# Key and value compression of the first mixer as one step on both column halves of the tensor engine, with a new order of steps

## The chip, the cores and the metric

The kernel runs on one core of one Trainium2 chip. The metric is the device time of one execution in microseconds, as the median of several runs; less is better.

## What is computed

The program takes 256 tokens of width 1024 through four transformer layers, each a mixer and a gated feed-forward network. The change touches the first mixer, which joins a retention with a sparse attention of eight heads. The sparse attention has three branches; one of them looks at compressed keys and values. Every compressed token covers 32 tokens and begins 16 after the one before it, so 256 tokens give 15 compressed ones for each of the two groups of heads:

```python
def nsa_compress(kv, pos_emb, w1, w2):
    B, G, S, d = kv.shape
    r = CMP_BLOCK // CMP_STRIDE
    parts = kv.reshape(B, G, S // CMP_STRIDE, CMP_STRIDE, d)
    n = S // CMP_STRIDE - r + 1
    blocks = jnp.concatenate([parts[:, :, j:j + n] for j in range(r)], axis=3)
    flat = (blocks + pos_emb.astype(jnp.float32)).reshape(B, G, n, CMP_BLOCK * d)
    return jax.nn.gelu(flat @ w1.astype(jnp.float32)) @ w2.astype(jnp.float32)
...
    k_cmp = nsa_compress(kvh(kc), pos_k, w1_k, w2_k)
    v_cmp = nsa_compress(kvh(vc), pos_v, w1_v, w2_v)
```

With a head width of 64, `flat` has 2048 columns, `w1` is 2048x64 and `w2` is 64x64. Keys and values have weights of their own.

## The kernel before

**The stream of products.** The program is eight stages: mixers are the even ones, feed-forward networks the odd ones. All large weights pass as one stream of chunks of 128x1024 floats or less. SP loads a chunk into one of four `raw` buffers; ACT copies it to `whi`, rounded (`split`, L2047); POOL subtracts to get the rest, `wlo` (`lo`, L2347), in pieces of 256 columns here; and PE multiplies the activations with both (`product`, L1063, L1064 and L1070). The split of a chunk waits for the end of the sixth chunk before it, and the load of a chunk for the low part of the fourth before it. A block of output columns is four chunks here (three in the third block, which is 280 wide). Its units are sorted by the half of the tokens, so four successive units use four chunks, and the next four use them again.

**The order of the rest.** All other work is cut into steps, called by two letters: `TT` turns keys, `TC` copies them, `CA` is the product with `w1`, `CB`, `CE` and `CD` are the gelu (DVE, ACT, DVE), `CF` is the product with `w2`, `CG` its copy, `SC` are scores, `MK` their maxima, `EX` exponentials, `NW` normed weights, `TR` their turn, `AV` the product with the values, `EV` the eviction of a block, `GD` and `GE` the gates. A table of numbers, `PLAN`, says after which unit of the stage each step stands; each engine walks through the table and issues the steps that are its own, in that order. `@0`, `@1`, `@2` behind a step names its lane of PSUM: A[0], A[1] or G[1]. So the table fixes what each engine has in front of what, and a step whose input isn't there stops all that stands behind it on its engine.

**The compression before.** `keys_copy` (L2173, L2174) writes the turned keys and values into `Z`, 128 partitions with six groups of 256 columns, three each for keys and values (the third holds the position terms). `compress_in` is issued twice, for keys (`kind` 0) in G[1] and for values in A[0], each as 16 matmuls of the 64 columns of `w1c` with 45 columns of `Z` that lie 16 floats apart:

```python
z = Z[:, 3 * kind:3 * kind + 3, 2 * m:2 * m + 225:16]
wt = w1c[:, kind, 64 * m:64 * m + 64]
o = e.matmul(tile[0:64, 0:45].rearrange("p (g i) -> p g i", g=3), wt, z, start=m == 0, stop=m == 15)
```

Both results stand in partitions 0 to 63, and each has its own gelu there. A matmul in float32 shows as two records in the trace.

Of the kernel before, what the change touches and what calls it, by code (L numbers as in the profile page):

```python
# [286 lines left out]
40: MK 0 1 0; NA 2 0 0; EX 0 1 0; EX 1 1 1
41: WH 2 0 0; NW 0 1 0; NW 1 1 1
43: WL 2 0 0; TR 0 1 0; CPA 0 1 0; TR 1 1 1; SC 0 1 1 @2; MK 0 1 1; AV 0 1 0
44: CPA 1 1 1; NO 0 1 0; EX 0 1 1; CPV 1 1 1; SC 2 1 0 @0; AV 1 1 1  # L290
45: EV 5 0; MK 2 1 0; NO 1 1 1; EX 2 1 0
46: NW 2 1 0; SC 2 1 1 @1; EV 5 1; TR 2 1 0; NW 0 1 1
47: MK 2 1 1; CPA 2 1 0; EX 2 1 1
48: NA 2 1 0; AV 2 1 0; WH 2 1 0; TR 0 1 1
49: NW 2 1 1; WL 2 1 0
50: EV 6 0; GS 0; CPA 0 1 1; TR 2 1 1; CPV 2 1 1; R2A 0; R2V 0; CPA 2 1 1
51: R1 0 @0
53: R3 0; AV 0 1 1; AV 2 1 1; R4 0; NO 0 1 1; NA 2 1 1; WH 2 1 1; WL 2 1 1; R5 0; EV 6 1; R1 1 @1; GS 1
54: R2A 1; GT 0; R2V 1; GT 1; R6 0; R3 1; R7 0
55: R4 1; R8 0  # L300
57: R5 1; R6 1; MT 2 @0
58: MH 2; R7 1; ML 2
59: R8 1
61: MT 3 @1
62: MH 3
# [6 lines left out]
0: -RES 1 1; -RES 0 1  # L312
1: -SQ 0 1; -SQ 1 1; -XT 0 1; -XH 0 1
# [5 lines left out]
11: -RS 0; DR 0; SI 0 0; DR 1  # L319
13: RV; RM  # L320
14: HM 0 0; HM 0 1
15: HH 0 0
16: HT 0 1; HL 0 0; GX 1; GA 1
17: HT 0 0; SG 1; HL 0 1; HH 0 1; UX 1; HU 1
# [287 lines left out]
24: EV 2 1
25: EX 0 1; TR 0 0
26: KT 1 @0; NW 0 1; KA 1; CPA 0 0
27: KV 1; TR 0 1; EV 3 0; CPV 0 1; SC 1 0 @0; CPA 0 1; AV 0 0; WH 0 0; TBM 2; WH 0 1; WL 0 0; MK 1 0; WL 0 1
28: SC 1 1 @1; AV 0 1; MK 1 1
30: LB 3; EX 1 1; EX 1 0
# [8 lines left out]
42: EX 2 1; TR 2 0; CPA 2 0; NW 2 1; MK 3 0
44: TR 2 1; SC 3 0 @1; EV 5 0; EX 3 0; AV 2 0
45: CPV 2 1; NW 3 0
46: WH 2 0; CPA 3 0; CPA 2 1; WL 2 0; EV 5 1
47: TR 3 0  # L630
48: SC 3 1 @0; AV 3 0; WH 2 1; AV 2 1; WH 3 0
# [55 lines left out]
70: RES 0 0; BN 0 0  # L687
74: RES 0 1; BN 0 1
92: RES 1 0; BN 1 0; AG 0
93: RS 0  # L690
94: AP 0 0
95: AP 1 0; RES 1 1; BN 1 1; AG 1; RS 1; AP 0 1; AP 1 1
# [41 lines left out]
def program(nc, a, out):  # L734
    ctx = ExitStack()
    with ctx:
# [40 lines left out]
        w2c = sb("w2c", [64, 256], F, e0)  # L777
# [1636 lines left out]
```

## Time and profile before

| | |
|---|---|
| runs | 1279.97, 1278.13 and 1278.50 us; median 1278.5 us |
| the profiled execution | 1279.67 us, of which 1277.9 us is the span from the first to the last instruction |
| PE busy | 1263.6 us (99%), weight loads 1059.1 us (83%) |
| POOL, ACT, DVE busy | 1030.2, 768.9 and 494.0 us |
| mean granted TensorE clock | 0.997 |

A profile has a page of sums, a chain of waits (who released whom, followed back from the last instruction), a list of waits by engine, a timeline of each engine, and a table of stretches with busy times and granted clock. PE is the tensor engine's matmul side and PEld its weight loads, DVE the vector engine, ACT the scalar engine, POOL the GpSimd engine, SP the engine that issues the loads. The end of a matmul is modelled: a row's time reaches over the start of the next, so the pace of a row of many records is its time less that of one record, divided by their number less one.

### The profile page before, as it was taken

To read this page: it belongs to the slowest core of one execution; us is meant where nothing else is said; L and a number is where in the kernel's file an instruction comes from. 1 tells how busy PE (TensorE), PEld (TensorE's weight loads), DVE (VectorE), ACT (ScalarE), POOL (GpSimd) and SP (SyncE) were. 2 spreads that over 40 slices of the span, in tenths; PEclk is the share of its full clock that TensorE was granted. 3 is DMA by queue.
4 is the path that set the end of the run, shared out by engine and by line. 5 is a ranking of instruction groups with operands and counts; after the bars stand their busy time and mean duration, and the time that the engine had idled before them with its cause. 6 is when DMAs were issued, how large, how long until landed. Compare 5 with 4: busy or idle time off the path is not lost.

```text
span 1277.9 us, 20392 instructions
## 1 busy us (share of the span) xinstructions
PE 1263.6 (99%) x7594; PEld 1059.1 (83%) x7594; DVE 494.0 (39%) x1096; ACT 768.9 (60%) x1481; POOL 1030.2 (81%) x874
## 2 busy tenths in 40 slices
PE   8999999999999999999999999999999999999997
PEld 7877888888887887888888888888888888888886
DVE  3465424331168862433104565133203345233302
ACT  7656676654688877666445675466534565556631
POOL 6666789878977668988889787798889878799874
PEclk9999999999999999999999999999999999999999
DMA  8443466556544336656556444576565644476652
GB/s 287 155 132 108 140 222 215 191 170 185 183 162 133 121 110 201 197 187 192 177 188 200 151 146 151 184 223 218 182 196 171 227 149 132 153 247 210 191 173 82
DMA packets 63122, 224.97 MB, mean 176 GB/s; under 512 B 7344, under 2 KB 7984, under 8 KB 63024
## 3 DMA queue, kind: packets, MB, share of 16 engines
q1 hardware_dynamic: 62736, 223.57, 54.3%
q8 instruction: 61, 1.00, 0.3%
q14 instruction: 37, 0.30, 0.1%
q10 hardware_dynamic: 288, 0.10, 0.0%
HBM read 222.59 MB, written 1.05 MB: 175 GB/s over the span
## 4 chain that ended last, share of the span: by engine, by line
PE 95%; DVE 2%; ACT 2%; issue 1%; DMA 0%; SPq 0%; DVEq 0%; ACTq 0%
PE G L1063 18%; PE G L1064 17%; PE G L1070 17%; PE G L1089 10%; PE A L1089 10%; PE A L1092 5%; PE G L1092 5%; PE A L1201 1%; PE A L1118 1%; PE A L1237 1%; DVE MX L1942 1%; PE A L1261 1%; DMA X<-in_x 0%; PE G L1201 0%; PE A L1361 0%
## 5 line engine op out<-in xcount | busy, mean ns | idle before, releaser
L2347 POOL TENSOR_TENSOR wlo<-raw,whi 128x256 fp32r<-128x256 f32 (+2 forms) x866 | 1020.6, 1215 | 230.1 <-ACT whi L2047 229.2
L2047 ACT ACTIVATE whi<-raw 128x1024 fp32r<-128x1024 f32 x403 | 422.0, 1057 | 194.7 <-PE G L1070 152.5
L1063 PE MATMUL G<-whi,xx 128*128 128x512 f32 (+1 forms) x560 | 225.9, 404 | 0.3
L1064 PE MATMUL G<-whi,xx 128*128 128x512 f32 (+1 forms) x560 | 217.3, 389 | 0.0
L1070 PE MATMUL G<-wlo,xx 128*128 128x512 f32 (+1 forms) x560 | 171.7, 388 | 0.0
L1089 PE MATMUL G<-xx,whi 128*128 128x512 f32 x576 | 144.6, 393 | 0.0
L1089 PE MATMUL A<-xx,whi 128*128 128x512 f32 x576 | 144.5, 393 | 0.0
L1063 PE MATMUL G<-whi,hh 128*128 128x512 f32 x352 | 137.5, 391 | 0.0
L1064 PE MATMUL G<-whi,hl 128*128 128x512 f32 x352 | 137.1, 389 | 0.0
L1063 PEld LDWEIGHTS G<-whi,xx 128*128 128x128 f32 x560 | 105.4, 188 | 24.5 <-issue 4.9
L1070 PEld LDWEIGHTS G<-wlo,xx 128*128 128x128 f32 x560 | 104.8, 188 | 22.5
L1064 PEld LDWEIGHTS G<-whi,xx 128*128 128x128 f32 x560 | 105.6, 188 | 18.3
L1089 PEld LDWEIGHTS A<-xx,whi 128*128 128x128 f32 x576 | 103.8, 189 | 18.8
L1089 PEld LDWEIGHTS G<-xx,whi 128*128 128x128 f32 x576 | 103.6, 189 | 18.5
L1070 PE MATMUL G<-wlo,hh 128*128 128x512 f32 x352 | 108.4, 389 | 0.0
L1092 PEld LDWEIGHTS G<-xx,wlo 128*128 128x128 f32 x576 | 78.6, 190 | 5.6
L1092 PEld LDWEIGHTS A<-xx,wlo 128*128 128x128 f32 x576 | 78.6, 190 | 5.6
L1092 PE MATMUL A<-xx,wlo 128*128 128x256 f32 x576 | 80.3, 282 | 0.0
L1092 PE MATMUL G<-xx,wlo 128*128 128x256 f32 x576 | 80.3, 282 | 0.0
L1070 PEld LDWEIGHTS G<-wlo,hh 128*128 128x128 f32 x352 | 66.1, 188 | 13.9
L1063 PEld LDWEIGHTS G<-whi,hh 128*128 128x128 f32 x352 | 66.1, 188 | 13.4
L1064 PEld LDWEIGHTS G<-whi,hl 128*128 128x128 f32 x352 | 66.1, 188 | 13.4
(394 smaller groups left out, 1502.2 us busy)
## 6 DMA issues: line engine op xcount, KB each, us to landing
raw<-in_g SPq DMA_DIRECT2D x88, 512.0 KB, 3.7
raw<-in_u SPq DMA_DIRECT2D x88, 512.0 KB, 3.7
raw<-in_d SPq DMA_DIRECT2D x88, 512.0 KB, 4.0
raw<-in_w_h SPq DMA_DIRECT2D x32, 512.0 KB, 3.6
raw<-in_w_e SPq DMA_DIRECT2D x24, 512.0 KB, 3.7
raw<-in_w_a SPq DMA_DIRECT2D x24, 512.0 KB, 3.7
raw<-in_w_b SPq DMA_DIRECT2D x24, 512.0 KB, 3.5
raw<-in_w_eo SPq DMA_DIRECT2D x8, 512.0 KB, 3.5
```

The lines of the kernel that those rows point to most:

```text
L1063: e.matmul(o, sh[:, kt, xs], whi[h][:, ws], start=u.first and j == 0, stop=False)
L1064: e.matmul(o, sl[:, kt, xs], whi[h][:, ws], start=False, stop=False)
L1070: m = e.matmul(o, sh[:, kt, xs], wlo[h][:, ws], start=False, stop=u.stop and final)
L1089: e.matmul(o[:, :], whi[h][:, 128 * kt:128 * kt + 128], xx[:, kt, :], start=kt == 0, stop=False)
L1092: m = e.matmul(o[:, 0:256], wlo[h][:, 128 * kt:128 * kt + 128], xx[:, kt, 0:256], start=False, stop=kt == u.kts[-1])
L1118: m = e.transpose(A[t][:, 512 * b + 128 * i:512 * b + 128 * i + 128], X[:, t, 512 * b + 128 * i:512 * b + 128 * i + 128], ident)
L1201: m = e.matmul(tile[:, at:at + nk], qs[i], ks[i], start=not mask, stop=True, skip_group_check=True)
L1237: m = e.transpose(tile[0:kp, (i * nb + b) * 128:(i * nb + b) * 128 + 128], s[:, 2 * i if key[0] == 4 else i, 128 * b:128 * b + kp], ident)
L1261: m = e.matmul(heads4(tile[64 * g:64 * g + 64, 0:256], 2), v, wt[:, g:4:2, b, :], start=b == 0, stop=b == nb - 1, skip_group_check=True)
L1942: m = e.tensor_copy(mixed[rows, :, :, rows], blocks[rows])
L2047: e.activation(whi[c % NH][:, 0:n], raw[c % NR][:, 0:n], ACT.Copy).then_inc(s_hi, 1)
L2347: m = e.tensor_tensor(wlo[c % NH][:, i:j], raw[c % NR][:, i:j], whi[c % NH][:, i:j].bitcast(F), ALU.subtract)
```

## The change

The compression is one step with one key. Its 32 matmuls alternate between keys, which write partitions 0 to 63, and values, which write 64 to 127 of the same PSUM tile. The gelu runs once on 128 partitions. The second weights of the values lie in partitions 64 to 127, and their result goes to the second bank of G[1]. Then the table is new for stages 0, 1, 6 and 7 (in stages 1 and 7 a few steps move by one unit, in stage 6 some steps of the attention). Stages 2 to 5 are the same.

```diff
-18: TT 2 @1; CA 0 @2; CB 0; CA 1 @0; TC 2; EV 2 0; CE 0; CD 0; CB 1; MK 1 0 0
-19: CD 1; CG 0; SC 1 0 0 @1
-20: CE 1
-21: CG 1; GD; MK 0 0 1; EV 2 1; GE; EX 1 0 0; TC 3; EX 0 0 1; CF 1; CF 0
-23: TT 3 @0; SC 0 0 1 @2
+18: TT 2 @1; CB 0; TC 2; EV 2 0; CD 0; CE 0; MK 1 0 0
+19: CA 0 @2; CG 0; EV 2 1
+21: MK 0 0 1; EX 1 0 0; GD; GE; SC 1 0 0 @1; TC 3; CF 0; EX 0 0 1; TT 3 @0
+22: SC 0 0 1 @2
...
-                    e.dma_start(w2c[:, 0:64], a["cw2k"]).then_inc(d_cw, 16)
-                    e.dma_start(w2c[:, 64:128], a["cw2k"]).then_inc(d_cw, 16)
-                    e.dma_start(w2c[:, 128:192], a["cw2v"]).then_inc(d_cw, 16)
+                    e.dma_start(w2c[0:64, 0:64], a["cw2k"]).then_inc(d_cw, 16)
+                    e.dma_start(w2c[0:64, 64:128], a["cw2k"]).then_inc(d_cw, 16)
+                    e.dma_start(w2c[64:128, 0:64], a["cw2v"]).then_inc(d_cw, 16)
...
             def compress_in(key):
-                _, kind = key
                 tile, _ = lane_of("CA", key)
                 lane_free("CA", key)
                 e.wait_ge(d_cw, 16 * CW_LOADS)
-                e.wait_ge(S["TC"], nth("TC", 0, kind))
+                for kind in range(2):
+                    e.wait_ge(S["TC"], nth("TC", 0, kind))
                 e.wait_ge(S["MB"], nth("MB", 0))
                 for m in range(16):
-                    z = Z[:, 3 * kind:3 * kind + 3, 2 * m:2 * m + 225:16]
-                    wt = w1c[:, kind, 64 * m:64 * m + 64]
-                    o = e.matmul(tile[0:64, 0:45].rearrange("p (g i) -> p g i", g=3), wt, z, start=m == 0, stop=m == 15)
+                    for kind in range(2):
+                        z = Z[:, 3 * kind:3 * kind + 3, 2 * m:2 * m + 225:16]
+                        o = e.matmul(tile[64 * kind:64 * kind + 64, 0:45].rearrange("p (g i) -> p g i", g=3),
+                                     w1c[:, kind, 64 * m:64 * m + 64], z, start=m == 0, stop=m == 15)
                 o.then_inc(S["CA"], 1)
 
             def compress_out(key):
-                _, kind = key
                 tile, w = lane_of("CA", key)
-                x = w[0][0:64, 0:30]
+                x = w[0][:, 0:30]
                 e.wait_ge(S["CD"], nth("CD", *key))
-                if kind == 0:
-                    m = e.matmul(tile[:, 0:30], w2c[:, 0:128], x, start=True, stop=True)
-                else:
-                    for g in range(2):
-                        m = e.matmul(tile[0:15, 64 * g:64 * g + 64], x[:, 15 * g:15 * g + 15], w2c[:, 128:192],
-                                     start=True, stop=True)
+                e.matmul(tile[:, 0:30], w2c[0:64, 0:128], x[0:64], start=True, stop=True)
+                for g in range(2):
+                    m = e.matmul(tile[0:15, 512 + 64 * g:576 + 64 * g], x[64:128, 15 * g:15 * g + 15], w2c[64:128, 0:64],
+                                 start=True, stop=True)
                 m.then_inc(S["CF"], 1)
...
-                x, u, bias = w[0][0:64, 0:30], tile[0:64, 64:94], w[0][0:64, 96:97]
+                x, u, bias = w[0][:, 0:30], tile[:, 64:94], w[0][:, 96:97]
...
-                x, u, v = w[0][0:64, 0:30], tile[0:64, 64:94], tile[0:64, 96:126]
+                x, u, v = w[0][:, 0:30], tile[:, 64:94], tile[:, 96:126]
...
-                if kind == 0:
-                    e.tensor_copy(CK[:, 0:30], tile[:, 0:30]).then_inc(S["CG"], 1)
-                else:
-                    e.tensor_copy(CK[0:15, 64:192], tile[0:15, 0:128]).then_inc(S["CG"], 1)
+                e.tensor_copy(CK[:, 0:30], tile[:, 0:30])
+                e.tensor_copy(CK[0:15, 64:192], tile[0:15, 512:640]).then_inc(S["CG"], 1)
```

The table moves instructions at three places that matter here. The first is PE between the third unit of the third block and the fourth (units 18 and 19 of the stage). `Z,w1c` is the product with `w1`; `whi,xx` and `wlo,xx` are units. Before:

```order
L1159 MATMUL A<-CN,PJ 128x128 x2
L1172 MATMUL G<-Z,w1c 64x45 x16
L1172 MATMUL A<-Z,w1c 64x45 x16
L1063 MATMUL G<-whi,xx 128x280
L1064 MATMUL G<-whi,xx 128x280
```

And now:

```order
L1152 MATMUL A<-CN,PJ 128x128 x2
L1056 MATMUL G<-whi,xx 128x280
L1057 MATMUL G<-whi,xx 128x280
...
L1063 MATMUL G<-wlo,xx 128x280 x3
L1165 MATMUL G<-Z,w1c 64x45 x32
```

The product with `w1` moved back by one unit, and its two rows became one.

The second place is PE at the end of the third block, with the product with `w2` (`W,w2c` and `w2c,W`) and the scores of a later branch (`MB,IB` and `KT,QT`). Before:

```order
L1196 MATMUL A<-MB,IB 128x2x128 x2
L1201 MATMUL A<-KT,QT 128x128 x4
...
L1070 MATMUL G<-wlo,xx 128x280 x2
L1184 MATMUL A<-w2c,W 15x64 x2
L1181 MATMUL G<-W,w2c 128x30
L1063 MATMUL G<-whi,xx 128x512
```

And now:

```order
L1063 MATMUL G<-wlo,xx 128x280 x2
L1187 MATMUL A<-MB,IB 128x2x128 x2
L1192 MATMUL A<-KT,QT 128x128 x4
L1173 MATMUL G<-W,w2c 128x30
L1175 MATMUL G<-w2c,W 15x64 x2
L1152 MATMUL A<-CN,PJ 128x128 x2
L1056 MATMUL G<-whi,xx 128x512
```

The scores came later by two units, to stand directly ahead of the product with `w2`, and the turn of the last keys came earlier, directly behind it.

The third place is ACT around the copies into `Z`, where `whi<-raw` is the split of a chunk. Before:

```order
L2060 ACTIVATE PJ<-G,SM 128x512
L2047 ACTIVATE whi<-raw 128x1024
L2173 ACTIVATE Z<-G 64x256
...
L2174 ACTIVATE Z<-A 64x255
L2047 ACTIVATE whi<-raw 128x1024 x2
L2176 ACTIVATE KT<-A 128x256
L2060 ACTIVATE PJ<-G,SM 128x280
L2183 ACTIVATE G<-G 64x30
L2047 ACTIVATE whi<-raw 128x1024
L2183 ACTIVATE A<-A 64x30
```

And now:

```order
L2048 ACTIVATE PJ<-G,SM 128x512
L2161 ACTIVATE Z<-A 64x256
...
L2162 ACTIVATE Z<-A 64x255
L2035 ACTIVATE whi<-raw 128x1024 x3
L2164 ACTIVATE KT<-A 128x256
L2048 ACTIVATE PJ<-G,SM 128x280
L2171 ACTIVATE G<-G 128x30
L2048 ACTIVATE PJ<-G,SM 128x280
```

The split of the first chunk of the fourth block moved from ahead of the eight copies to behind them; the exponential of the gelu is one. On POOL and SP no row moves.

## Rows read from the trace of the kernel before

**Rows 1.** The page: span, shares of the chain that ended last.
```profile
span 1277.9 us, 20392 instructions
...
PE 95%; DVE 2%; ACT 2%; issue 1%; DMA 0%; SPq 0%; DVEq 0%; ACTq 0%
```

**Rows 2.** The two longest waits of PE (us in total, times, longest).
```profile
PE A L1118 <- DMA X<-in_x: 2.2, 2, 1.1
PE A L1337 <- ACT QK L2272: 1.8, 1, 1.8
```

**Rows 3.** Timeline of PE, 36 to 49 us: start us, us, line, out<-in, shape, count.
```profile
36.49 2.73 PE L1172 MATMUL G<-Z,w1c 128*64 128x45 f32 x32
39.04 2.71 PE L1172 MATMUL A<-Z,w1c 128*64 128x45 f32 x32
41.68 0.40 PE L1063 MATMUL G<-whi,xx 128*128 128x280 f32 x1
...
42.95 0.39 PE L1196 MATMUL A<-MB,IB 128*128 128x256 bf16 x2
43.27 0.71 PE L1201 MATMUL A<-KT,QT 64*128 64x128 f32 x8
43.92 0.40 PE L1063 MATMUL G<-whi,xx 128*128 128x280 f32 x1
...
45.18 0.30 PE L1063 MATMUL G<-whi,xx 128*128 128x280 f32 x1
...
46.05 0.39 PE L1184 MATMUL A<-w2c,W 64*15 64x64 f32 x4
...
46.71 0.50 PE L1063 MATMUL G<-whi,xx 128*128 128x512 f32 x1
...
48.22 0.39 PE L1063 MATMUL G<-whi,xx 128*128 128x512 f32 x1
```

**Rows 4.** Timeline of PE, three later stretches: halves, then strips of the array.
```profile
382.26 0.51 PE L1361 MATMUL G<-W 128*32 128x32 f32 x35
...
1021.93 1.09 PE L1266 MATMUL G<-W,PJ 128*64 128x128 f32 x16
1022.95 0.50 PE L1063 MATMUL G<-whi,xx 128*128 128x512 f32 x1
```

**Rows 5.** Timeline of DVE, 39 to 49 us: the gelu of the keys, the gates.
```profile
39.25 0.15 DVE L1554 COPY W<-G 64x1 f32<-64x1 f32 x1 [12.49 <-PE G L1172]
...
41.69 0.18 DVE L1575 TENSOR_TENSOR W<-G,W 64x30 f32<-64x30 f32 x1
...
47.12 1.39 DVE L1589 TENSOR_SCALAR SM<-PJ 128x24 f32<-128x24 f32 x2
```

**Rows 6.** Timeline of ACT, 33 to 42 us: splits and copies into Z.
```profile
33.49 1.05 ACT L2047 ACTIVATE whi<-raw 128x1024 fp32r<-128x1024 f32 x1
34.44 0.36 ACT L2173 ACTIVATE Z<-G 64x256 f32<-64x256 f32 x1
...
37.17 0.38 ACT L2174 ACTIVATE Z<-A 64x255 f32<-64x255 f32 x1
37.57 2.00 ACT L2047 ACTIVATE whi<-raw 128x1024 fp32r<-128x1024 f32 x2
...
40.88 0.17 ACT L2183 ACTIVATE G<-G 64x30 f32<-64x30 f32 x1 [0.51 <-DVE G L1565]
```

**Rows 7.** Timeline of POOL, 34 to 50 us: the low parts of the weights.
```profile
34.62 2.81 POOL L2347 TENSOR_TENSOR wlo<-raw,whi 128x256 fp32r<-128x256 f32 x4 [1.54 <-ACT whi L2047]
38.71 11.17 POOL L2347 TENSOR_TENSOR wlo<-raw,whi 128x256 fp32r<-128x256 f32 x16 [1.28 <-ACT whi L2047]
```

**Rows 8.** Stretches of 2 us: busy PE, PEld, DVE, ACT, POOL, then PEclk.
```profile
406.00:408.00 2.00, 1.83 (x9) 1.66 (x10) 1.97 (x5) 1.97 (x4) 0.88 (x2) 0.79 0.00 0
408.00:410.00 2.00, 2.00 (x31) 1.18 (x33) 1.09 (x4) 1.06 (x3) 1.93 (x3) 0.50 0.02 4
410.00:412.00 2.00, 2.00 (x52) 1.72 (x44) 1.23 (x4) 2.00 (x4) 0.00 (x0) 0.85 0.48 133
```

More of the change, by code:

```diff
@@ L287 @@
[L287 to L305, printed above, removed]
+37: NW 2 0 0; CPA 1 1 0; AV 2 0 1; RO 1 1; NO 1 1 0; AV 1 1 0; TR 2 0 0
+39: WH 2 0 1; NA 2 0 1; WL 2 0 1; CPA 2 0 0; SC 1 1 1 @1; SC 0 1 0 @0; MK 1 1 1; AV 2 0 0
+40: EX 0 1 0; NA 2 0 0; MK 0 1 0; EX 1 1 1
+41: NW 0 1 0; NW 1 1 1; WH 2 0 0
@@ new lines @@
+42: TR 0 1 0; CPA 0 1 0
+43: WL 2 0 0; AV 0 1 0; TR 1 1 1
+44: SC 2 1 0 @0; SC 0 1 1 @2; CPA 1 1 1; NO 0 1 0; AV 1 1 1; CPV 1 1 1
+45: EV 5 0; EX 2 1 0; MK 2 1 0; MK 0 1 1; EX 0 1 1; NO 1 1 1; SC 2 1 1 @1; TR 2 1 0
+46: NW 2 1 0; NW 0 1 1; EV 5 1; MK 2 1 1; CPA 2 1 0; AV 2 1 0
+48: EX 2 1 1; NA 2 1 0; TR 0 1 1
+49: WL 2 1 0; NW 2 1 1; WH 2 1 0
+50: EV 6 0; GS 0; TR 2 1 1; CPA 0 1 1; CPV 2 1 1; R2A 0; R2V 0; CPA 2 1 1
+51: R4 0; R1 0 @0
+53: NO 0 1 1; R3 0; AV 0 1 1; AV 2 1 1; NA 2 1 1; WH 2 1 1; WL 2 1 1; R5 0; EV 6 1; R1 1 @1; GS 1
@@ L306 @@
+54: R2A 1; R2V 1; GT 0; R7 0; R3 1; R6 0; GT 1; R4 1
+55: R8 0
+56: R5 1; R6 1; MT 2 @0
+57: MH 2
+58: ML 2
+59: R8 1; R7 1
+61: MH 3; MT 3 @1
 63: ML 3
-65: RES 0 0; SQ 0 0; XT 0 0; RES 1 0
-66: XH 0 0; XT 1 0; XL 0 0; XH 1 0
+65: RES 0 0; XT 0 0; RES 1 0; SQ 0 0
+66: XH 0 0; XL 0 0; XT 1 0
+67: XH 1 0
 68: XL 1 0
@@ L318 @@
 10: -SQ 1 0
[L319 to L324, printed above, removed]
+11: DR 0; -RS 0; SI 0 0; DR 1
+13: RV; HM 0 0; RM
+15: HM 0 1; HH 0 0
+16: GX 1; HL 0 0; GA 1; HT 0 0
+17: SG 1; UX 1; HL 0 1; HT 0 1; HH 0 1; HU 1
 18: HB 1; HW 1; GX 2; GA 2
@@ L606 @@
 13: EV 1 0
-15: EV 1 1; SC 0 1 @2; SC 0 0 @1
-16: MK 0 0
-17: MK 0 1; EX 0 0
+15: EV 1 1; SC 0 1 @2; SC 0 0 @1; MK 0 0; EX 0 0
+17: MK 0 1
 19: NW 0 0; LB 2
 20: EV 2 0
[L612 to L617, printed above, removed]
+21: EX 0 1
+24: EV 2 1; TR 0 1
+25: TR 0 0
+26: KT 1 @0; NW 0 1; CPA 0 0; KA 1
+27: KV 1; CPA 0 1; EV 3 0; CPV 0 1; AV 0 0; AV 0 1; SC 1 0 @0; WH 0 0; WH 0 1; TBM 2; WL 0 0; MK 1 0; WL 0 1; SC 1 1 @1; MK 1 1
+30: EX 1 1; LB 3; EX 1 0
 33: EV 3 1; NW 1 1
@@ L622 @@
 37: KV 2; WL 1 1
-39: SC 2 1 @2; SC 2 0 @0; EV 4 1; MK 2 0; KT 3 @1
+39: SC 2 0 @0; SC 2 1 @2; EV 4 1; MK 2 0; KT 3 @1
 40: EX 2 0
 41: KA 3; MK 2 1; NW 2 0; KV 3
[L626 to L631, printed above, removed]
+42: EX 2 1; TR 2 0; CPA 2 0; NW 2 1
+43: MK 3 0; EV 5 0
+45: CPV 2 1
+46: SC 3 0 @1; EX 3 0; AV 2 0; TR 2 1; WH 2 0; CPA 2 1; CPA 3 0; NW 3 0; WL 2 0; EV 5 1
+48: TR 3 0; SC 3 1 @0; AV 3 0; WH 2 1; AV 2 1; WH 3 0
 49: MK 3 1
 50: WL 2 1
-51: EX 3 1; WL 3 0; NW 3 1
+51: WL 3 0; EX 3 1; NW 3 1
 58: TR 3 1; RES 0 0
@@ L686 @@
 52: HB 18; HW 18; TBL
[L687 to L690, printed above, removed]
+74: RES 0 0; RES 0 1; BN 0 1
+75: BN 0 0
+91: RES 1 0
+92: BN 1 0; AG 0; RS 0; AP 1 0
 94: AP 0 0
-95: AP 1 0; RES 1 1; BN 1 1; AG 1; RS 1; AP 0 1; AP 1 1
+95: RES 1 1; BN 1 1; RS 1; AG 1; AP 0 1; AP 1 1
 """,
@@ L776, in program @@
         w1c = sb("w1c", [128, 2, 16 * 64], F, e0)
-        w2c = sb("w2c", [64, 256], F, e0)
+        w2c = sb("w2c", [128, 128], F, e0)
         CK = sb("CK", [128, 512], F, e0)
@@ L1550, in gelu_argument @@
                 tile, w = lane_of("CA", key)
-                x, u, bias = w[0][0:64, 0:30], tile[0:64, 64:94], w[0][0:64, 96:97]
+                x, u, bias = w[0][:, 0:30], tile[:, 64:94], w[0][:, 96:97]
                 k = -2.0 * (2.0 / np.pi) ** 0.5
                 e.wait_ge(S["CA"], nth("CA", *key))
-                e.tensor_copy(bias, tile[0:64, 30:31]).then_inc(s_dve, dv.up())
+                e.tensor_copy(bias, tile[:, 30:31]).then_inc(s_dve, dv.up())
                 own()
-                e.tensor_scalar(x, tile[0:64, 0:30], bias, None, ALU.add).then_inc(s_dve, dv.up())
+                e.tensor_scalar(x, tile[:, 0:30], bias, None, ALU.add).then_inc(s_dve, dv.up())
                 own()
```

59 lines of the change are left out of this document (26 added, 33 removed).

## The prediction

> **What bounds the kernel now.** I read the page first: the span is 1277.9 us, and the chain that ended last runs through PE for 95% of it [rows 1]. PE is busy for 1263.6 us of the span. The list of PE's waits is short: the first loads, 2.2 us in all, and one wait for copies by ACT in the third stage, 1.8 us [rows 2]. None lies in the first mixer once it runs. So a microsecond that PE does not have to issue is a microsecond of time, work that goes from DVE or ACT is worth nothing by itself, and a new wait of PE costs its full length. That is why the timeline of PE comes next [rows 3], and then, for every step that PE will wait on, the timelines of DVE, ACT and POOL [rows 5, 6, 7].
>
> **The product with the first weights, before.** It holds PE from 36.49 to 41.68 us, 5.19 us for 64 records [rows 3]. The pace of a record is (2.73 - 0.26) / 31 = 0.080 us, where 0.26 is about one record's own time. So 63 paces are 5.0 us, and leaving for the next unit the rest.
>
> **The same, on two halves.** A record on the left half and one on the right may run side by side. The trace has this form: 16 records of 128 columns on alternating halves take 1.09 us, so their pace is (1.09 - 0.27) / 15 = 0.055 us, or 0.109 for a pair [rows 4]. Four strips of 32 columns show it more strongly: 35 records in 0.51 us are a pace of (0.51 - 0.20) / 34 = 0.009 us [rows 4], or 0.28 ns a column, less than the 0.42 ns of one clock at 2.4 GHz, so streams must run side by side there. In our case each half still has to take its own 32 records, and the only pace seen for such a record is 0.080. A pair then costs 0.080, and 32 pairs 2.55 us. Ends: the 16 records of the halves keep PE from 1021.93 to 1022.95, 1.02 us, against 16 x 0.055 = 0.87, so 0.15 us [rows 4]. Together 2.70 us, and **the saving is 5.19 - 2.70 = 2.5 us**. Bounds: without any overlap 64 x 0.080 + 0.15 = 5.3 us, no saving at all; if a half were as quick per column as the pairs of 128, 0.109 x 45/128 = 0.038 for a pair, 1.2 + 0.15 us, a saving of 3.8. I take 2.5, since the single stream is the nearest row and it has the same stride and the same weights.
>
> There is a rule that speaks against this part. The Trainium skill, page "TensorEngine Tiling (Array Packing)", section "Performance Considerations", says that every matmul carries some 60 cycles of overhead, that few columns are no quicker than 60, and that one should not take the factor from a dimension that is already small. Our 45 columns are such a dimension. If that overhead were paid one record after the other, the product would stay at 5.3 us and the time at 1278.6 us. By that rule, the trace does not agree for the strips, which stream 32 columns at 0.009 us a record [rows 4].
>
> **Joined and parted steps.** A run of row or column halves costs PE its ends: eight records of the scores at a pace of (0.71 - 0.27) / 7 = 0.063 are 0.50 us, but they hold it from 43.27 to 43.92, 0.65 us [rows 3]. So 0.15 us a run. The product with the second weights stood alone from 46.05 to 46.71 [rows 3] and now follows the scores directly: one run fewer. One product with the values stands alone now (one more), and in stage 6 two runs of halves became one (one fewer). Net -0.15 us, with bounds of -0.4 and +0.2.
>
> **Off the path.** DVE drops 9 small operations and ACT one exponential; PE never waited for them, so 0. The loads of w2c are the same three; SP and POOL keep their order: 0. Stages 1 and 7 move steps by a unit with no wait of PE near: 0.
>
> **What PE may now wait for.** Four places.
> - The product with w1 needs all eight copies into Z. They took from 34.44 to 37.55 us behind a split that began at 33.49 [rows 6]; without that split ahead they begin some 0.2 us sooner and end at 37.3. PE comes there one unit later than before, at 36.49 + 1.27 = 37.7 (a unit of nine records holds 41.68 to 42.95) [rows 3]. Slack 0.3 us.
> - The gelu took DVE and ACT from 39.25 to 41.87 = 2.62 us [rows 5]. PE has ahead of the second product: a unit of nine (1.27), a unit of six (46.05 - 45.18 = 0.87) and scores (43.92 - 42.95 = 0.97), 3.1 us, less the tail of the last matmul, 0.26 [rows 3]. Slack 0.2 us. ACT must be free when the exponential comes: its three splits after 37.3 end at 40.3, and a copy and an eviction at 41.1; the exponential comes at about 42.2. Free.
> - The split of the first chunk of the fourth block ends at 38.3 us, behind the copies, and not at 34.5. POOL stood idle for it before; now its four chunks of four pieces, at 11.17 / 16 = 0.70 us a piece [rows 7], are done at 38.3 + 11.2 = 49.5. PE begins that block at 46.71 - 2.4 = 44.3, needs up to 1.51 us a unit [rows 3], and comes to the low part of the fourth chunk at about 44.3 + 4.2 + 0.5 (scores) + 0.9 = 49.9. Slack 0.4 us, where it was over 5.
> - The clamp of the gates, 1.39 us [rows 5], comes behind the maxima of the second scores on DVE. Between 0 and 1.39 us of it may show; I expect nearer 0, as the first turn of weights stands three units later.
>
> Three slacks of 0.2 to 0.4 us and one unknown: I add 0.2 us, bounds 0 and 1.4.
>
> **Sum.** -2.5 - 0.15 + 0.2 = -2.4 us. Against the profiled execution (1279.67 us; 1.8 of it lies outside the span) that is 1277.3. The median of the runs shown is 1278.5, 1.2 lower. What differs is likely the clock: after PE's wait of 1.8 us the granted clock fell, 0.79, 0.50 and 0.85 of 2.4 GHz in three stretches of 2 us [rows 8], a loss of 0.4 + 1.0 + 0.3 = 1.7 us, and the two lower runs are 1.2 and 1.5 us under the profiled one. The Trainium skill, page "TensorE: Matmul & The Clock Gate", Part 1, has two such levels, half and full rate; the trace agrees with its 0.50 in one stretch. So I take the median as the base: **1276.1 us**, 0.19% less. A difference under 0.2%, 2.6 us, can't be told from none, and the forecast lies just inside.
>
> **Rivals.**
> - *The halves do not overlap for this operand.* Z is read 16 floats apart, and 0.080 us for 45 columns is slow beside 0.109 for a pair of 128. If the stride sets the pace and both halves share the reading, a pair costs 0.16 and nothing is gained: 1276.1 + 2.5 = 1278.6 us. For it: no strided stream runs in halves in this trace. Against it: the strips read four streams at once [rows 4]. The Trainium skill, page "SBUF — State Buffer", section "Door 1", says that elements in a new 16-byte line each pay a penalty; that explains 0.080, and does not say whether two streams pay it twice. Chance 0.14; with the fixed overhead above, 0.03 more.
> - *The clock is at half speed in the median run.* The wait of 1.8 us stays [rows 2], and a fall after it costs 1.7 us: 1277.8 us. It may have been in one run of three before. Chance 0.18.
> - *Slower: the weights come late.* The mechanism is POOL's debt. It starts 3.7 us later into four chunks that it works at 2.8 us each, while PE uses them at 1.4 us each [rows 3, 7]. If a split waits for ACT by more than the slack of 0.4 us, PE waits for the low part in the fourth unit, the next loads (each bound to an old low part) come late too, and each of the four blocks behind pays: 4 x 1 us, and with a fall of the clock 1.7: 1276.1 + 5.7 = 1281.8. It decides from 5.0 us of waits on, since 2.4 are saved. Against it: POOL is idle later in every block, when chunks wait for PE. Chance 0.07.
>
> **How the numbers follow.** The forecast has 0.58, the rivals 0.17, 0.18 and 0.07. The forecast's own cases reach from 1275.9 without any wait to 1276.6; its centre is 0.16 us from the bound of 0.2%, so I give 0.38 of its 0.58 to faster and 0.20 to the same, for the base may be a little high or low. The first rival is no change (0.17), the second too (0.15 of 0.18, 0.03 faster). So faster 0.41, same 0.52, slower 0.07. The range reaches down to 1274.8 (the saving of 3.8 us on the product instead of 2.5) and up to 1279.3 (the first rival with half of the bound of the waits, 0.7); outside lie the slower rival and parts of the others, under 0.2.
>
> **What would show it.** Right: one row of 64 records on halves in G, about 2.7 us long, with pairs of starts; no wait of PE for Z, for the gelu or for a low part between 36 and 60 us; the fourth block beginning at 44.3. Wrong: a row of about 5 us (first rival), a wait of PE for DVE at the product with w2, or a granted clock under 1.00 elsewhere. If POOL's debt counts, PE's waits name POOL's line near 50 us.

## The result and the profile after

The changed kernel takes **1281.39 us** in the median of 16 executions (1280.44 to 1287.19) where the kernel before takes 1279.15 (16 executions, 1278.13 to 1281.61). The ratio is 1.0023, with a 95% interval of 1.0016 to 1.0030: slower by 0.2%, where 1276.1 us was forecast. Two of the sixteen lie at 1286.3 and 1287.2, and one at 1283.8; the highest of the kernel before is 1281.61. The profiled execution took 1281.39 us, and its span is 1279.6 us, 1.7 more than before [rows 1].

Below, line numbers are those of the changed kernel: 7 to 9 less than before in PE's part, 9 to 12 less in those of DVE, ACT and POOL.

The edit itself did what it was meant to. PE's timeline of the changed kernel, the same stretch as [rows 3]:

```profile
37.59 2.83 PE L1165 MATMUL G<-Z,w1c 128*64 128x45 f32 x64
40.34 0.40 PE L1056 MATMUL G<-whi,xx 128*128 128x280 f32 x1
...
43.27 0.30 PE L1173 MATMUL G<-W,w2c 64*128 64x30 f32 x2
43.50 0.39 PE L1175 MATMUL G<-w2c,W 64*15 64x64 f32 x4
...
44.02 0.48 PE L1056 MATMUL G<-whi,xx 128*128 128x512 f32 x1
```

The product with w1 holds PE from 37.59 to 40.34, 2.75 us and not 5.19, and the next block begins at 44.02 where it was to begin at 44.3. Compared product by product, PE is 2.9 us ahead of the kernel before at 52 us and still at 404 us, in the middle of stage 2; under 0.1 us of that stood already ahead of the product with w1. Then it loses it all. PE's longest waits in the changed kernel, which answer to [rows 2]:

```profile
PE A L1328 <- ACT QK L2260: 5.9, 1, 5.9
PE G L1097 <- DVE PJ L1414: 1.0, 1, 1.0
PE A L1111 <- DMA X<-in_x: 1.0, 1, 1.0
```

The wait for the copies QK was 1.8 us and is 5.9. The stretches of 6 us around it in the changed kernel (busy PE, PEld, DVE, ACT, POOL, then PEclk), where [rows 8] showed 0.79, 0.50 and 0.85 in stretches of 2 us:

```profile
400.00:406.00 6.00, 1.52 (x7) 0.94 (x5) 5.90 (x18) 3.48 (x10) 0.00 (x0) 1.00 0.22 82
406.00:412.00 6.00, 4.55 (x31) 3.51 (x35) 4.32 (x10) 4.21 (x14) 2.79 (x4) 0.53 0.00 1
412.00:418.00 6.00, 6.00 (x139) 5.16 (x131) 3.81 (x10) 5.23 (x7) 3.40 (x5) 0.90 0.26 90
418.00:424.00 6.00, 6.00 (x158) 5.17 (x146) 4.05 (x11) 4.77 (x18) 6.00 (x10) 1.00 0.63 182
```

The two stretches behind the wait miss 6 x (0.47 + 0.10) = 3.4 us of full clock, twice the 1.7 us of [rows 8]. Of the 1.7 us more, 1.1 show in the shift of the products behind it. So the account is -2.9 (stage 0), +4.1 (the wait), +1.1 (the clock) and -0.6 (stage 6, where the new order has fewer ends of runs; which edit there gives it was not tried apart) = +1.7 us, the difference of the spans.

Whose work is late? The chain of waits of the changed kernel, from 390 us to PE's restart (start, us, what), names it:

```profile
389.84 0.32 DVE G L1835
390.15 0.29 issue
390.45 8.47 DVE MX L1930
398.94 0.22 DVE MX L1930
...
402.48 0.10 ACT lf L2245
...
405.40 2.00 ACT QK L2260 x11
407.41 0.04 issue
407.45 0.58 PE A L1328
```

L1930 (1942 before) is `diagonal_blocks`, called DB here: VectorE copies four blocks of 32 partitions x 128 elements from one SBUF tile (DG) to another (MX). One of them takes 8.47 us. The line by itself, before and then changed (ns min/median/max, first and last start):

```profile
L1942 DVE COPY MX<-DG x16: 202/683/2929, 393.3 to 465.9; 32x128 f32<-32x128 f32 x16
```

```profile
L1930 DVE COPY MX<-DG x16: 202/223/8475, 390.4 to 468.2; 32x128 f32<-32x128 f32 x16
```

It was in the trace of before, unread: sixteen equal copies whose shortest takes 202 ns and whose longest 2929. Beside them GpSimd makes low parts of weights in one unbroken run. Its timeline, before and changed:

```profile
382.16 19.57 POOL L2347 TENSOR_TENSOR wlo<-raw,whi 128x256 fp32r<-128x256 f32 x28 [3.52 <-ACT whi L2047]
```

```profile
379.30 19.55 POOL L2335 TENSOR_TENSOR wlo<-raw,whi 128x256 fp32r<-128x256 f32 x28 [3.53 <-ACT whi L2035]
```

A piece takes 19.55 / 28 = 0.70 us, four make a slice. In the changed kernel the copy comes at 390.45, where the 17th piece begins (379.30 + 16 x 0.698 = 390.47), is held for twelve pieces, and ends at 398.92, just behind the run (398.85). Before, it came at the same piece (393.30, against 382.16 + 16 x 0.699 = 393.34) and was held for four only, to 396.23. Everything before that point has moved by the same 2.85 us, and yet the one copy is held for three times as long. That is what the experiments are about.

### The profile page after: what moved, and what is told of

Read it like the earlier page. It is cut to its first block, busy times and chain, and to the rows that moved or that the text cites. A ratio compares the mean times of both kernels' runs of the same rounds, so it can differ in the third digit from the quotient of the medians.

```text
span 1279.6 us, 20380 instructions
## 1 busy us (share of the span) xinstructions
PE 1262.3 (99%) x7594; PEld 1058.7 (83%) x7594; DVE 497.1 (39%) x1087; ACT 769.7 (60%) x1480; POOL 1029.9 (80%) x874
## 4 chain that ended last, share of the span: by engine, by line
PE 92%; ACT 2%; DVE 2%; POOL 2%; DMA 1%; issue 1%; SPq 0%; DVEq 0%; ACTq 0%
PE G L1056 17%; PE G L1057 17%; PE G L1063 17%; PE G L1082 10%; PE A L1082 10%; PE A L1085 5%; PE G L1085 5%; POOL wlo L2335 1%; PE A L1192 1%; PE A L1111 1%; PE A L1228 1%; DVE MX L1930 1%; ACT whi L2035 1%; PE A L1252 1%; DMA X<-in_x 0%
```

## The experiments

Each time is the median of a kernel's executions, taken on the same chip as a series of the kernel before. Theory A: the copy can't run beside GpSimd's subtractions, and its length is PE's wait. Rivals: the copy only reports a delay that ScalarE or a DMA makes; the length of the hold is a matter of the phase of arrival.

### Another form of the copy: e1 to e4

```
-  m = e.tensor_copy(mixed[rows, :, :, rows], blocks[rows])
+  m = e.tensor_tensor(mixed[rows, :, :, rows], blocks[rows], blocks[rows], ALU.max)
```

In e1 and e2 for all four blocks, in e3 and e4 for the first block only.

> The changed kernel, with the four copies of the step DB on VectorE (the diagonal blocks, 32 partitions x 128 elements, from SBUF to SBUF) written as the maximum of the block and itself: same values, same place in the order. In the changed kernel's profile these four take 9.17 us in stage 2 (one of them 8475 ns), and it ends when GpSimd's unbroken run of 28 subtractions ends; TENSOR_TENSOR steps of the same stretch run beside GpSimd at their usual length. Theory A (a plain copy inside SBUF cannot run beside a GpSimd instruction, and this copy holds up PE): the four take about 1 us, TensorE's wait of 5.9 us for QK in stage 2 is under 0.5 us, its clock doesn't fall at 417 us, and the time is 1281.4 - 5.9 - 3.4 = 1272.1 (1271.5 to 1274). Theory B (the wait comes from the late slice of weights or from ScalarE's evictions, and the copy only reports it): the wait stays between 4 and 6 us and the time between 1280.5 and 1282. Theory C (the four are slow in any form, since GpSimd takes the reads): four instructions of some 0.7 us each and more, time 1276 to 1281.

> The kernel before with the same edit of DB. There the four took 5.03 us, PE waited 1.8 us, and the clock was at half for 3.4 us. Theory A: the wait of 1.8 us and the clock's fall both go: 1279.15 - 1.8 - 1.7 = 1275.6 (1275.2 to 1277.5). Against the changed kernel with this edit it then is 2.5 to 2.9 us slower, since the saving of the change (2.85 us in the shift of every product of stages 0 and 1) is no longer given back. Theory B: 1278.5 to 1280, and the changed kernel with the edit stays slower than this one. Theory C: 1277 to 1279.

> The changed kernel with only the first of DB's four blocks as a maximum, the other three still as copies. The first copy then comes some 0.2 us later, in the middle of a GpSimd subtraction and not 8 ns ahead of one. Theory A with chance (a copy gets in only when it happens to be first at the end of a GpSimd instruction): the time held up changes by whole subtractions of 0.70 us; it may be anything from 0.7 to 8.5 us, and the time lies between 1274 and 1282, and the three copies' excess and PE's wait go together one for one. Theory D (the copy always waits till GpSimd's run of 28 ends, whatever its arrival): the first copy again ends at the run's end, about 398.9 us, and the time is 1281 to 1282.

> The kernel before with only the first of DB's four blocks as a maximum. There the first copy waited for four subtractions (2.93 us) and each later one for one (0.69 us). Theory A with chance: a different number of whole subtractions; 0.2 us of arrival can change the time by several us in either direction (1275.5 to 1283). Theory D: the three copies end with GpSimd's run, at about 401.7 us, PE's wait grows by about 4 us and the time is 1283 to 1285. A smooth dependence (the copy costs what it did less one of four): 1278.3 to 1279.

Measured: e1 1287.22 us (1282.22 to 1288.56), e2 1280.11, e3 1287.15, e4 1278.54, beside 1279.65 before. All expectations of theory A for e1 and e2 were missed. In e3 the hold ends with GpSimd's run, as theory D said, but the time is 5 us over its 1282; in e4 it does not, and the time is that of the smooth dependence. The line in e1's profile says why theory A was missed:

```profile
L1930 DVE TENSOR_TENSOR MX<-DG x16: 261/288/8549, 396.8 to 474.2; 32x128 f32<-32x128 f32 x16
```

A maximum of two operands in SBUF is held exactly as the copy is. The twelve and the four come again with their kernels: e1 and e3 (changed) have 8549 ns, e2 and e4 (before) 3006 and 2994. So this change of the operation does not end the hold. The phase was not varied by it: in all four the first instruction comes within 0.03 us of the start of the 17th piece, as in the two kernels without the edit. What settles the phase is e11 and e14, further down.

e1 and e3 are also 6 us longer than the changed kernel, through something earlier. PE's second wait in e1, and what DVE and POOL do ahead of it:

```profile
PE A L1228 <- DVE W L1678: 4.0, 1, 4.0
```

```profile
47.42 5.59 DVE L1577 TENSOR_SCALAR SM<-PJ 128x24 f32<-128x24 f32 x2
```

```profile
39.00 13.89 POOL L2335 TENSOR_TENSOR wlo<-raw,whi 128x256 fp32r<-128x256 f32 x20 [4.30 <-ACT whi L2035]
```

That is the clamp of the gates, a tensor_scalar inside SBUF that took 1.39 us in [rows 5]. In e1 its first instruction is held for 5507 ns, till GpSimd's run of twenty pieces in stage 0 ends (39.00 + 13.89 = 52.89 us), and the weights of the local attention wait behind it. PE waits 4.0 us, and behind that the granted clock is 0.50 from 56 to 58 us and 0.67 from 58 to 60, a loss of 1.7: together the 6 us. It would explain the few executions of the changed kernel that lie some 5 us higher (none of them has a profile); e13 and e15 put that to the test. DB comes 340 us behind the clamp, so the edit of e1 and e3 cannot be what holds it; what makes five of six executions of e1, and all five of e3, have the long hold was not found.

### A form with one input: e5 and e6

```
-  m = e.tensor_copy(mixed[rows, :, :, rows], blocks[rows])
+  m = e.tensor_reduce(mixed[rows, :, :, rows], blocks[rows].unsqueeze(4), X_AX, ALU.add)
```

> The changed kernel with DB's four copies written as a reduction over an axis of length 1 (one SBUF input, same values). The maximum form of the first call was held up just like the copy (8549 ns), while the TENSOR_REDUCE of the blocks that runs in the same stretch, from SBUF to SBUF beside GpSimd's subtractions, takes 520 ns and is never longer. Theory A, made narrower (a plain copy or tensor_scalar inside SBUF and any VectorE instruction with two SBUF inputs is held while GpSimd runs; one with a single input outside these is not): the four take about 1 us together, PE's wait for QK in stage 2 is under 0.5 us in place of 5.9, its clock doesn't fall behind it, and a run in which the clamp of the gates (a tensor_scalar inside SBUF, 47 us) is not held long comes to 1281.4 - 5.9 - 3.4 = 1272.1 (1271.5 to 1274.5); a run in which it is held for 5.5 us, as in e1, is 4 to 5 us longer. Theory E (it is ScalarE's or the DMA's timing that makes PE wait, and any form of DB shows it): the wait stays over 4 us and the time at 1281.

> The kernel before with the same reduction for DB. Theory A: PE's wait of 1.8 us for QK goes and so does the half clock behind it: 1279.15 - 1.8 - 1.7 = 1275.6 (1275 to 1277). The changed kernel with this edit is then 2.5 to 3.5 us faster than this one, which is what the change saves by itself. Theory E: 1278.5 to 1280.

Measured: e5 **1272.96 us** (ratio to before 0.9957, 0.9942 to 0.9972), e6 1276.26 us (0.9978, 0.9968 to 0.9987). The line in e5:

```profile
L1930 DVE TENSOR_REDUCE MX<-DG x16: 261/276/284, 396.7 to 464.9; 32x128 f32<-32x128 f32 x16
```

Sixteen instructions between 261 and 284 ns, beside the same run of GpSimd. PE's wait for QK is gone from both lists, and the granted clock is 1.00 from 406 to 424 us in both. In the kernel before that is worth 2.9 us in the medians (2.3 against the 1278.58 taken beside e6) and 3.6 in PE's products (a shift of +0.3 us ahead of it and -3.3 behind): 3.1 right behind the wait, for its 1.8 and most of the 1.7 of clock, and 0.5 more by 500 us. In the changed kernel it is worth 1281.39 - 1272.96 = 8.4 us. The profiled execution of e5 is the one of its seven that took 1278.94 us: in it the clamp is held for 5492 ns, PE waits 4.0 us behind that, and the clock falls behind the wait as in e1, which is the 6 us over the others. Theory A holds in its narrower form, and the rival that blames ScalarE or a DMA falls: neither was touched.

The Trainium skill, page "SBUF — State Buffer", section "Who interferes with whom", has this rule: VectorE and GpSimd share one pair of SBUF ports, which one instruction locks as a whole; a copy or tensor_scalar in a two-port mode wants it, so does a VectorE instruction with two SBUF inputs while GpSimd reads, and a tensor_reduce never does. The runs agree in all four forms: copy 8475 ns, tensor_scalar 5507, maximum 8549, reduction at most 284. How many of GpSimd's instructions the waiting side has to let pass, the rule does not say.

### Four pieces or twelve: e7, e8, e11, e14

Before the change, ScalarE's high part of the sixth slice of that run was ready at 395.98 us (it began at 394.93, below) and GpSimd took it up at 396.10. Changed, it was ready at 392.85, and GpSimd took it up at 393.25, 0.4 us later. The difference is a hole of 0.29 us ahead of ScalarE's activation L2244, which the kernel before has and the changed one has not. ScalarE's timeline, before and changed:

```profile
393.76 0.60 ACT L2244 ACTIVATE W<-G 128x512 f32<-128x512 f32 x1 [0.29 <-issue]
394.39 0.60 ACT L2246 ACTIVATE G<-W 128x512 f32<-128x512 f32 x1
394.93 2.13 ACT L2047 ACTIVATE whi<-raw 128x1024 fp32r<-128x1024 f32 x2
```

```profile
391.80 1.05 ACT L2035 ACTIVATE whi<-raw 128x1024 fp32r<-128x1024 f32 x1
393.15 1.06 ACT L2035 ACTIVATE whi<-raw 128x1024 fp32r<-128x1024 f32 x1 [0.29 <-PE G L1063]
```

The expectation of e11 takes the 0.29 us in the changed kernel for the same hole at a later place. The rows name another cause: before, nothing that the profile shows ends it ("issue"); changed, the split of the seventh slice waits for the end of a unit on PE. In all traces of the changed kernel and its variants the activation that answers to L2244 starts 12 to 16 ns behind the one ahead of it, and in all of the kernel before 289 or 290 ns.

Theory G: a held instruction gets in only where GpSimd itself must stop, if only for an instant; here that is the boundary between two slices, if the next high part is just ready. e7 and e8 make GpSimd stop at every slice, e11 makes the high part late by more work on ScalarE, e14 stops GpSimd at this one boundary (slice 123).

e7 and e8, and e14 with the condition `if c == 123` ahead of the new wait:

```
 e.wait_ge(s_hi, c + 1)
+e.wait_ge(s_lo, c)
```

e11:

```
+for i in range(0, 896 if c == 123 else 0, 128):
+    e.activation(whi[c % NH][:, i:i + 128], raw[c % NR][:, i:i + 128], ACT.Copy)
+i = 896 if c == 123 else 0
-e.activation(whi[c % NH][:, 0:n], raw[c % NR][:, 0:n], ACT.Copy).then_inc(s_hi, 1)
+e.activation(whi[c % NH][:, i:n], raw[c % NR][:, i:n], ACT.Copy).then_inc(s_hi, 1)
```

> The changed kernel, DB as it was; GpSimd waits before each slice's subtractions until its own subtractions of the slice before are done, so that its run has a gap every four pieces (2.8 us). In the traces so far VectorE's held copy got in only where a slice's high part was ready 0.12 us before GpSimd needed it (before) and not where it was ready 0.4 us ahead (changed). If GpSimd's unbroken issue is what keeps the copy out: no held instruction is longer than 3.0 us; DB takes at most 5 us as before, the clamp of the gates at most 3; time 1274 to 1278. If the number of subtractions that it waits for has another cause: one of 8.5 us again, and 1281 to 1282.5.

> The kernel before with the same wait of GpSimd for its own last slice. The copy there was already let in after one slice (2.93 us), so by the theory nothing changes but the gaps of some 0.05 to 0.1 us per slice on GpSimd: 1278 to 1280. Where GpSimd's throughput were the bound of a stage it would be slower: over 1281.

> The changed kernel, DB and clamp as they were, with more work on ScalarE: the high part of one slice (the one whose split began at 391.80 us and ended at 392.85, 0.4 us before GpSimd began its low part at 393.25) is made in eight pieces, so that it ends 0.3 to 0.6 us later. Theory G (the held copy gets in only where GpSimd must itself wait, or nearly, for a slice's high part; in the kernel before that part was ready 0.12 us ahead because of a hole of 0.29 us in ScalarE's issue, which in the changed kernel lies one instruction later): the first copy of DB is held for four subtractions (2.8 to 3.0 us) and not for twelve (8.5), DB takes 5 us, PE's wait falls from 5.9 to 1.8 us, its half clock from 6.8 to 3.4 us, and the kernel with more work is 4 to 6 us faster: 1275.5 to 1277.5. Rival (the number of subtractions depends on something else, such as the phase of the arrival): 8.5 us again and 1281 to 1282.

> The changed kernel with one wait more and nothing else: before the slice whose subtractions begin at 393.25 us in stage 2 GpSimd waits for its own subtractions of the slice before. Theory G (unbroken issue over that boundary keeps the copy out): the first copy of DB is held for four subtractions, 2.8 to 3.0 us, in place of twelve; PE's wait falls from 5.9 us to 0.8 to 1.8; the lower level of the times is 1274 to 1276.5, that is 5 to 7 us under the changed kernel, for a wait that costs GpSimd under 0.2 us. Rival: the copy is held for twelve again and the time stays at 1281 to 1282.

Measured: e7 1276.83 us, e8 1280.31; e11 1274.30, with seven executions at 1273.8 to 1274.3 and five at 1279.65 to 1279.9; e14 three at 1274.4 to 1275.0 and nine at 1280.4 to 1281.8. The step DB in VectorE's timelines of e11 and e14, which took 9.17 us in the changed kernel:

```profile
390.70 4.07 DVE L1930 COPY MX<-DG 32x128 f32<-32x128 f32 x4
```

```profile
390.60 4.50 DVE L1930 COPY MX<-DG 32x128 f32<-32x128 f32 x4
```

GpSimd's run in the same two:

```profile
379.56 13.98 POOL L2338 TENSOR_TENSOR wlo<-raw,whi 128x256 fp32r<-128x256 f32 x20 [3.51 <-ACT whi L2038]
393.88 5.66 POOL L2338 TENSOR_TENSOR wlo<-raw,whi 128x256 fp32r<-128x256 f32 x8 [0.34 <-ACT whi L2038]
```

```profile
379.41 19.79 POOL L2337 TENSOR_TENSOR wlo<-raw,whi 128x256 fp32r<-128x256 f32 x28 [3.51 <-ACT whi L2035]
```

The first copy is held for 2922 and 2887 ns, four pieces, as theory G said. And it comes at the same phase as ever, by the 17th piece: 390.70 us against 379.56 + 16 x 0.699 = 390.74 in e11, 390.60 against 379.41 + 16 x 0.698 = 390.58 in e14. With the phase kept and the hold gone from twelve pieces to four, the phase falls as the reason. In e11 more work on ScalarE makes the kernel 7.1 us faster at its lower level (1281.39 against 1274.3); in e14 one wait of GpSimd, which lengthens its run of 28 pieces by 0.24 us (19.79 for 19.55), takes PE's wait down to 1.3 us, and the lower level is 6.4 to 7 us under the changed kernel. The expected 5 to 7 us of e14 were right. The 4 to 6 of e11 were exceeded: PE's wait is 0.8 us and not 1.8, since two of the three later copies take 0.22 us and not 0.69, and the clock does not fall behind it. The median of e14 is still 1280.81 us, no better than the kernel before, for nine of its twelve executions are at the upper level. e7 shows that waits at every slice end both holds (the longest DB copy 731 ns, the clamp 0.49 us in all) but cost some 4 us elsewhere (e7 against e5 3.9, e8 against e6 4.1): in e7 PE waits 0.9 us for a low part at 28 us and loses 2 us more for VectorE at 500 and 975 us. e8 is 0.3 us over the 1280 that were expected at most.

So a stop of GpSimd ends the hold: that is shown. That the 0.12 us against the 0.4 make the difference between the two kernels has no test but e11, where the high part was so late that GpSimd stood still for 0.34 us; before, no stop shows in its row. What makes the hole of 0.29 us ahead of L2244 was not tried.

### The clamp: e9, e10, e13, e15

e9 and e10 have DB as in e5, and the clamp with its output given as 3 x 8 columns.

```
-  e.tensor_scalar(gates[:, 24 * t:24 * t + 24], ...
+  e.tensor_scalar(gates[:, 24 * t:24 * t + 24].rearrange("p (a b) -> p a b", a=3), ...
```

> The changed kernel with DB as a reduction (as in e5) and with the clamp of the gates given its output as 3 x 8 columns and its input as 24: the same values in the same place, in a form of the operands that two ports could not halve. In e5 one of seven runs was at 1278.9 and had the clamp held for 5.5 us; the other six were at 1272.7 to 1273.0. Theory A (both are one mechanism): both clamps take 0.15 to 0.25 us each, PE's wait of 4.0 us for the local attention's weights is never seen, and every run lies between 1272.3 and 1273.5, 6 us under the changed kernel with 8 us off the upper end of its scatter. Rival F (the clamp is held in this form too, so its being held is not a matter of the second port): it shows 0.65 us and more, and some runs at 1278 to 1279 again.

> The kernel before with the same two edits. The clamp was held for 0.69 and 0.78 us there, never for longer in the profiles so far, and PE waited for nothing behind it: 1276.3 as e6 (1275.8 to 1276.6). The pair with e9 gives the change alone, without the held instructions: 3.3 us (2.9 to 3.6), of which 2.85 us in stage 0 and the rest in stage 6.

Measured: e9 1273.29 us with one of nine executions at 1280.0, e10 1276.25. The clamp in e9 still has 648 and 783 ns: rival F was right that this form is held too. Three columns of eight lie side by side, so they may have become one of 24 again on the way to the chip; that is open. As a pair, e10 and e9 give the change alone: 1276.25 - 1273.29 = **3.0 us** in the medians, and 3.35 us in the last products of the two traces, of which 2.75 come from stage 0 and 0.6 from stage 6.

e13 has DB as in e5 and lets GpSimd stop at the pieces beside the clamp; e15 has VectorE as it was and only pauses of GpSimd, those of e13 and that of e14 (123 is added to the first list).

```
+  if c in (14, 15, 16):
+      e.wait_ge(s_lo, c)
   for i, j in zip(cuts, cuts[1:]):
       m = e.tensor_tensor(wlo...)
+      if c in (14, 15) and j < n:
+          m.then_inc(s_pl, 1)
+          e.wait_ge(s_pl, 3 * (c - 14) + j // 256)
```

> The changed kernel with DB as a reduction, and with GpSimd waiting for its own last piece before each of the next ones in the three slices of stage 0 beside which the clamp of the gates comes (from 46.7 to 53 us), and nowhere else. Theory A: the clamp is held for at most one piece (0.9 us for each of its two instructions), PE never waits for the local attention's weights, no execution lies at the upper level of 1278 to 1280 and all lie within 1272.5 to 1273.8. If the upper level has another cause, one execution in four to nine is again 6 us longer.

> The changed kernel with VectorE's work untouched and pauses of GpSimd alone: the one of e14 in stage 2, and those of e13 beside the clamp of the gates in stage 0. In e14, 9 of 12 executions were at the upper level (1280.4 to 1281.8) and 3 at the lower (1274.4 to 1275.0). If the upper level is the clamp held behind GpSimd's unbroken run, no execution is at it any more, and all lie between 1274.2 and 1276. If it has another cause, most are at 1280 to 1282 again.

Measured: e13 **1273.27 us**, all five within 1273.10 to 1273.55 (ratio to before 0.9952, 0.9939 to 0.9965). e15 1274.92 us, all six within 1274.87 to 1275.41 (0.9966, 0.9954 to 0.9979), where nine of twelve executions of e14 lay 6 us higher. So the upper level is the clamp, held. e13 and e15 beat both kernels, and e15 does it with pauses alone.

Two things stay open. How often the long hold comes differs with no cause found: e14 has it in nine of twelve executions, the changed kernel at most in three of sixteen, and the two do not differ ahead of stage 2. And the "only" of theory G is too strong. The clamp by itself, in e5 and then in e9:

```profile
L1577 DVE TENSOR_SCALAR SM<-PJ x2: 166/2829/5492, 47.3 to 52.7; 128x24 f32<-128x24 f32 x2
```

```profile
L1577 DVE TENSOR_SCALAR SM<-PJ x2: 648/716/783, 47.1 to 47.7; 128x24 f32<-128x24 f32 x2
```

In both it comes 0.12 us behind the start of the 13th piece. In e5 it is held for eight pieces, to the run's end; in e9 it gets in behind that one piece, in the middle of a slice, where GpSimd waits for nothing.

### Do the halves overlap only in turn: e12

```
-  for m in range(16):
-      for kind in range(2):
+  for kind in range(2):
+      for m in range(16):
```

> e9 with the product with w1 in two rows of 32-column-half products, first the 16 of the keys and then the 16 of the values in each of their groups, and not in turn on the two halves. If two halves of the array overlap only when neighbouring products go to different halves (the saving of the change is that overlap): the 64 products take 5.1 us in place of 2.8 and the time is that of e9 plus 2.3: 1275.1 (1274.8 to 1275.6). If the saving comes from something else (the shared group, fewer waits): the same as e9 within 0.3 us.

Measured: 1277.12 us, 3.8 above e9 where 2.3 were expected. PE's timeline has the product itself as forecast, 39.34 to 44.24, 4.9 us for the same 64 records:

```profile
39.34 4.96 PE L1165 MATMUL G<-Z,w1c 128*64 128x45 f32 x64
```

So 2.15 us (4.90 - 2.75) of it is the overlap, which needs neighbours on different halves. The other 1.7 fit the clamp once more: 3.40 us for its two instructions in this profile, and PE waits 1.8 us for the weights behind it, at a granted clock that stays at 1.00. The profiled execution is the longest of the eleven, 1278.49 us: its clock was 0.50 from 10 to 12 us, so its product begins 1.5 us later than in e9 (39.34 against 37.83). Whether the clamp is held as long in the other ten is not shown.

## Why the prediction was wrong

**The product on two halves: right.** 2.70 us were forecast, 2.75 measured; the saving is 2.44 against 2.5. e12 shows that it is the overlap of neighbours. The rival "the halves do not overlap for this operand" is refuted, and so is the reading that a fixed overhead is paid one record after the other.

**Joined and parted steps: right in sign, small in size.** -0.15 with a bound of -0.4; measured -0.3 in stage 0 (2.75 of shift less 2.44 of the product) and -0.6 in stage 6, so -0.9.

**What PE may now wait for: right in the profiled execution.** No wait for Z, for the gelu or for a low part of the fourth block appears before 400 us; the rival of POOL's debt did not come. "The clamp of the gates, 1.39 us ... Between 0 and 1.39 us of it may show" holds there too: the clamp takes 1.35 us and PE waits for nothing behind it. It fails as a bound: the length was taken from one profile as if it were the work's own. It is 0.17 us of work for each half and else waiting for GpSimd, and the hold reached 5.5 us in e1 and e5. The prediction worked out when GpSimd is done with four chunks, 49.5 us, and not that its run goes on unbroken behind them: the changed kernel's run in stage 0 is 24 pieces to 55.1 us, where one of 16 ended at 49.9 [rows 7], so that a clamp of 47 us can be held for 8 us and not for 2.8.

```profile
38.44 16.66 POOL L2335 TENSOR_TENSOR wlo<-raw,whi 128x256 fp32r<-128x256 f32 x24 [5.51 <-ACT whi L2035]
```

That this later end is what made the upper level appear was argued from these rows, not tried apart.

**The step that failed: stage 2 costed at nothing.** The second rival says it outright: "The wait of 1.8 us stays [rows 2]". The forecast took everything behind stage 1 as shifted by a constant, its waits included, and no term of its sum stands for stage 2. But the wait of 1.8 us was itself made of a hold of 2.93 us on DB's first copy. The hold depends on whether GpSimd's run has a stop at the right slice, and it went from four pieces to twelve: +4.1 us of wait and +1.1 of clock, against -3.5 saved. With that step taken out of both kernels the change is worth 3.0 to 3.3 us (e10 and e9, e6 and e5), 0.6 to 0.9 more than the 2.4 forecast.

**The base.** That the clock makes the difference between the executions before is borne out by e4, profiled at 1278.29 us. PE's wait there is the same as in [rows 2], and the granted clock is 1.00 from 400 to 418 us:

```profile
PE A L1337 <- ACT QK L2275: 1.8, 1, 1.8
```

So a wait of 1.8 us need not bring a fall, and the 1.4 us between this execution and the profiled one before are about its 1.7. The base was 0.65 us low all the same: of the sixteen executions before eight lie at 1278.13 to 1278.91 and eight at 1279.39 to 1281.61, and their median of 1279.15 falls between. The rival "the clock is at half speed in the median run" took a fall in one run of three; by these levels it is about one in two. Of the rivals' signs, the slower side was right, by luck: the mechanism was not the one priced but a longer hold of an instruction on another engine, two stages behind the edit.

## What to carry to other kernels

Where the wait that a shift is assumed to keep is made by one instruction, look at that instruction's shortest and longest time: equal shapes with 202 and 2929 ns are not work but a hold, and a hold need not shift with the rest. A VectorE copy, a tensor_scalar inside SBUF or an instruction with two SBUF inputs on the way to PE should not stand beside a long unbroken run of GpSimd; a reduction over an axis of length 1 did the same copy in 0.28 us, and a wait of GpSimd for its own last instruction at the right place was worth 6 us for 0.24, in the executions in which the clamp was not held as well. When an edit gives less than its own rows say, undo the hold in both versions and compare again: here that turned +0.2% into -0.2%.

## What the runs showed of the hardware

- A VectorE instruction that is held by GpSimd is not always let in at the next instruction's end: 2.9, 5.5 and 8.5 us for an instruction of 0.2 us, while GpSimd did 4, 8 and 12 subtractions. With the same arrival the clamp was let in behind one piece in e9 and behind eight in e5. Once the first copy was in, its three successors were held for one piece each or none (0.22 to 0.69 us).
- It is let in where GpSimd waits for a semaphore, even where the wait hardly shows in GpSimd's timeline: the pieces of e14 stand in one row of 28, 0.24 us longer than the changed kernel's.
- ScalarE stood idle for 0.29 us ahead of one activation of stage 2 in all six traces of the kernel before and its variants, with nothing in the profile that ends it, and for 12 to 16 ns in all traces of the changed kernel and its variants. The cause is open.
- Behind waits of PE of 0.8 and 1.3 us the granted clock stayed at 1.00. Behind 1.8 us it was at its half level for 3.4 us in all in the kernel before, and stayed at 1.00 in e4 and e12. Behind 4.0 us (e1, e5) the half level held for 3.4 us, and behind 5.9 us for 6.8.
- Two streams of 64 weight columns and 45 moving columns on the two halves of the array run at about the pace of one when they alternate (0.043 us a record), and at 0.077 when they do not.
